# Modulation columns of the first layer in four quarters of two blocks, and the first four units computed two blocks at a time

## What is computed

```python
cond = jax.nn.silu(c.astype(jnp.float32))
mod = cond @ ada_w[i].astype(jnp.float32) + ada_b[i].astype(jnp.float32)
shift, scale, gate = jnp.split(mod[:, None, :], 3, axis=-1)
h = (rms_norm_f32(x, norm_g[i]) * (1.0 + scale) + shift).astype(x.dtype)
...
proj = h @ w_in
q, k, v, g = jnp.split(proj, [RET_QK_WIDTH, 2 * RET_QK_WIDTH, 2 * RET_QK_WIDTH + RET_WIDTH], axis=-1)
```

## Time and profile before

| | us |
|---|---|
| median of 3 runs | 1806.66 |
| lowest and highest | 1804.52, 1806.71 |
| profiled execution, its own time | 1805.74 |
| span of the profiled execution | 1803.9 |
| TensorE busy | 1763.1 (98% of the span) |
| VectorE, ScalarE, GpSimd busy | 931.5, 471.5, 1103.0 |

### The profile page before, as it was taken

How to read it: one execution, slowest core, us unless ns; L and a number is a source line. 1 busy time by engine, 2 the same in 40 slices (tenths; PEclk the granted TensorE clock), 3 DMA queues, 4 the chain that set the end, 5 groups by cost and what they waited for, 6 DMA issues and landing times.

```text
span 1803.9 us, 26195 instructions
## 1 busy us (share of the span) xinstructions
PE 1763.1 (98%) x9198; PEld 1477.0 (82%) x9198; DVE 931.5 (52%) x1534; ACT 471.5 (26%) x958; POOL 1103.0 (61%) x848
## 2 busy tenths in 40 slices
PE   6999999999999999999999999989989999999998
PEld 4888888888888888888888778877878878888887
DVE  4754736574455545555443888786373463213311
ACT  4121221200233222322221247555332422002200
POOL 3656555698455444645457659864066588667863
PEclk9999999999999999999999999999999999999999
DMA  9523222385232222332223322200022333333331
GB/s 359 171 77 94 84 73 76 93 302 166 62 105 81 77 76 77 92 91 76 75 77 104 96 73 59 59 24 25 24 82 76 88 95 103 101 98 88 99 99 54
DMA packets 281588, 172.87 MB, mean 96 GB/s; under 512 B 6000, under 2 KB 272560, under 8 KB 280496
## 3 DMA queue, kind: packets, MB, share of 16 engines
q1 hardware_dynamic: 275024, 151.01, 28.5%
q10 hardware_dynamic: 6496, 20.93, 3.4%
HBM read 169.69 MB, written 2.10 MB: 95 GB/s over the span
## 4 chain that ended last, share of the span: by engine, by line
PE 92%; DVE 6%; SPq 1%; ACT 1%; DMA 0%; issue 0%; DVEq 0%; ACTq 0%
PE acc L390 14%; PE acc L392 14%; PE acc L391 14%; PE ob L390 4%; PE ob L392 4%; PE ob L391 4%; PE acc L420 3%; PE acc L422 3%; PE acc L421 3%; PE sc L1622 2%; PE acc L438 2%; PE acc L439 2%; PE acc L440 2%; PE sc L1543 1%; PE ob L1634 1%; PE acc L2035 1%
## 5 line engine op out<-in xcount | busy, mean ns | idle before, releaser
L766 POOL TENSOR_TENSOR wl<-raw,wh 128x512 fp32r<-128x512 f32 x456 | 638.6, 1421 | 19.3
L763 POOL TENSOR_SCALAR wh<-raw 128x1024 fp32r<-128x1024 f32 (+1 forms) x232 | 268.4, 1157 | 571.2 <-PE acc L392 143.5
L390 PE MATMUL acc<-hh,wh 128*128 128x512 f32 x800 | 325.6, 407 | 1.2 <-ACT sq L1413 1.2
L392 PE MATMUL acc<-hh,wl 128*128 128x512 f32 x800 | 313.7, 392 | 0.0
L391 PE MATMUL acc<-hl,wh 128*128 128x512 f32 x800 | 312.8, 391 | 0.0
L390 PEld LDWEIGHTS acc<-hh,wh 128*128 128x128 f32 x800 | 151.3, 189 | 35.5 <-issue 2.6
L391 PEld LDWEIGHTS acc<-hl,wh 128*128 128x128 f32 x800 | 151.5, 189 | 32.3 <-issue 2.4
L392 PEld LDWEIGHTS acc<-hh,wl 128*128 128x128 f32 x800 | 150.9, 189 | 33.0
L390 PE MATMUL ob<-Yh,wh 128*128 128x512 f32 x256 | 100.5, 393 | 0.0
L392 PE MATMUL ob<-Yh,wl 128*128 128x512 f32 x256 | 99.7, 390 | 0.0
L391 PE MATMUL ob<-Yl,wh 128*128 128x512 f32 x256 | 99.7, 389 | 0.0
(11 more groups left out here) (545 smaller groups left out, 3725.7 us busy)
## 6 DMA issues: line engine op xcount, KB each, us to landing
raw<-in_att_w_in SPq DMA_DIRECT2D x64, 512.0 KB, 4.0
raw<-in_mlp_w SPq DMA_DIRECT2D x64, 512.0 KB, 3.9
raw<-in_ret_w_in SPq DMA_DIRECT2D x48, 512.0 KB, 3.7
ada_w<-in_ada_w ACTq DMA_DIRECT2D x8, 1536.0 KB, 7.0
raw<-in_w_in SPq DMA_DIRECT2D x23, 512.0 KB, 3.6
ada_w<-in_ada_w SPq DMA_DIRECT2D x16, 512.0 KB, 8.9
raw<-in_ret_w_out SPq DMA_DIRECT2D x16, 512.0 KB, 4.3
raw<-in_att_w_out SPq DMA_DIRECT2D x16, 512.0 KB, 4.0
```

The source lines that it names most:

```text
L390: e.matmul(bank[:, :], wh[:, s, k, :], rhs_high(k), start=(start and k == 0), stop=False)
L392: last = e.matmul(bank[:, :], wl[:, s, k, :], rhs_high(k), start=False, stop=(stop and k == k1 - 1))
L763: e.tensor_scalar(wh[:, s, 0:k1, :], raw[:, s, 0:k1, :], 1.0, 1.0, ALU.mult, ALU.mult).then_inc(high_done, 1)
L766: low = e.tensor_tensor(wl[:, s, k0:k0 + KT // 2, :], raw[:, s, k0:k0 + KT // 2, :], wh[:, s, k0:k0 + KT // 2, :].bitcast(F32), ALU.subtract)
```

## The change

The four parts are cut another way: part n now holds scale and shift of blocks 2n and 2n+1, 256 columns each. Each of the 16 transfers of 512 KB becomes two of 256 KB with rows of 1 KB. A part then gives both modulation vectors of two blocks (`ada_mod` with one addition over both and one gain). The loads of units 0 and 1 now both stand ahead of part 1, unit 2 ahead of part 2, and parts 2 and 3 follow one another. On TensorE the first four units are cut in pieces of two blocks. All columns go to the bank `st`, and `ada_turned(n)` waits for `mod0` of n-1.

```diff
             def load_ada0(n):
-                part, k0 = ADA_PART[n]
                 for j in range(KT // 2):
-                    e.dma_start(ada_w0[n][:, 2 * j:2 * j + 2, :],
-                                rows(ins["ada_w"][0], 2 * j, 2 * j + 2, part * D + k0 * P, S)).then_inc(ada_in[n][j], 16)
+                    for half in range(2):
+                        e.dma_start(ada_w0[n][:, 2 * j:2 * j + 2, half * 256:(half + 1) * 256],
+                                    rows(ins["ada_w"][0], 2 * j, 2 * j + 2, (1 - half) * D + 2 * n * P, 256))\
+                         .then_inc(ada_in[n][j], 16)
...
-            for n in range(1, 4):
-                load_ret(0, (n - 1,))
-                load_ada0(n)
+            load_ret(0, range(2))
+            load_ada0(1)
+            load_ret(0, (2,))
+            load_ada0(2)
+            load_ada0(3)
             load_ret(0, range(3, 6))
...
             ada_turned(0)
             norm_spread(e, "n0")
             ada_rows(1)
+            first_unit(0, 0, 2)
+            ada_turned(1)
+            first_unit(1, 0, 2)
+            ada_rows(2)
+            first_unit(0, 2, 4)
+            ada_turned(2)
+            first_unit(1, 2, 4)
+            ada_rows(3)
             e.wait_ge(*AC.at(f"x{2 * NT - 1}"))
-            ada_turned(1)
-            first_unit(0, 0, 4)
-            ada_rows(2)
-            ada_rows(3)
-            ada_turned(2)
-            first_unit(1, 0, 4)
+            first_unit(2, 0, 4)
             ada_turned(3)
-            first_unit(2, 0, 4)
             for j in range(3):
-                first_unit(j, 4, KT)
-            first_unit(3, 0, KT)
+                first_unit(j, 4, 6)
+            first_unit(3, 0, 6)
+            for j in range(4):
+                first_unit(j, 6, KT)
...
-            for k in range(4):
-                normed(k)
-            ada_mod(1)
-            for k in range(4):
-                low(k)
-            ada_mod(2)
-            for k in range(4, KT):
-                normed(k)
-            ada_mod(3)
-            for k in range(4, KT):
-                low(k)
+            for n in range(4):
+                if n:
+                    ada_mod(n)
+                for k in range(2 * n, 2 * n + 2):
+                    normed(k)
+                for k in range(2 * n, 2 * n + 2):
+                    low(k)
```

More of the change, by code:

```diff
@@ L223, in build @@
         ada_w0 = [at(f"ada_w0{n}", [P, KT, S], n * 16 * KB) for n in range(4)]
-        ADA_PART = [(1, 0), (0, 0), (1, 4), (0, 4)]
         ada_g0 = at("ada_g0", [P, KT, D], 0)
@@ L880, in _ @@
             e.activation(cos_[:, :], tmp[:, 1, :], ACT.Sin).then_inc(*AC.done("rope"))
-            ada_rows(1)
-            e.wait_ge(*V.at("mod01"))
             for k in range(KT):
-                if k == 4:
-                    ada_rows(2)
-                    ada_rows(3)
-                    e.wait_ge(*V.at("mod03"))
+                if k and k % 2 == 0:
+                    ada_rows(k // 2)
                 e.wait_ge(*V.at(f"n0t{k}"))
@@ L1437, in _ @@
                     last.then_inc(*PE.done(f"x{2 * t + half}"))
-            mod_bank = [st, ob[1], st, ob[1]]
             def ada_rows(n):
@@ L1446, in ada_rows @@
                     if k % 2 == 0:
-                        e.wait_ge(ada_in[n][k // 2], 16)
+                        e.wait_ge(ada_in[n][k // 2], 32)
                     g = k % 4
@@ L1453, in ada_turned @@
             def ada_turned(n):
-                part, k0 = ADA_PART[n]
-                c = part * KT + k0
                 e.wait_ge(*AC.at(f"rows{n}"))
-                if n >= 2:
-                    e.wait_ge(*V.at(f"mod0{n - 2}"))
+                if n:
+                    e.wait_ge(*V.at(f"mod0{n - 1}"))
                 for j in range(4):
-                    last = e.matmul(mod_bank[n][:, c + j:c + j + 1], sq[:, n % 2, j * P:(j + 1) * P], qk_gain[:, 2:3],
+                    c = (1 - j // 2) * KT + 2 * n + j % 2
+                    last = e.matmul(st[:, c:c + 1], sq[:, n % 2, j * P:(j + 1) * P], qk_gain[:, 2:3],
                                     start=True, stop=True)
@@ L1481, in _ @@
             ada_rows(1)
-            e.wait_ge(*AC.at(f"x{2 * NT - 1}"))
-            ada_turned(1)
-            first_unit(0, 0, 4)
-            ada_rows(2)
-            ada_rows(3)
-            ada_turned(2)
-            first_unit(1, 0, 4)
+            first_unit(0, 0, 2)
[6 more added lines that the diff above has]
+            ada_rows(3)
+            e.wait_ge(*AC.at(f"x{2 * NT - 1}"))
+            first_unit(2, 0, 4)
             ada_turned(3)
-            first_unit(2, 0, 4)
             for j in range(3):
-                first_unit(j, 4, KT)
-            first_unit(3, 0, KT)
+                first_unit(j, 4, 6)
+            first_unit(3, 0, 6)
+            for j in range(4):
+                first_unit(j, 6, KT)
             def ret_values(i, u, c):
@@ L2373, in _ @@
             roots(e, 0, NT, "n0root")
-            mod_bank = [st, ob[1], st, ob[1]]
             def ada_mod(n):
-                part, k0 = ADA_PART[n]
-                c = part * KT + k0
+                k0 = 2 * n
                 e.wait_ge(*PA.at(f"cols{n}"))
[L2381 to L2385, removed]
+                m = mod[:, 0, 0:2, k0:k0 + 2]
+                step(e, e.tensor_tensor(m, st[:, 0:2 * KT].rearrange("p (a k) -> p a k", a=2)[:, :, k0:k0 + 2],
+                                        sm("ada_b0", 0, 2 * KT).rearrange("p (a k) -> p a k", a=2)[:, :, k0:k0 + 2],
+                                        ALU.add), V, f"mod0{n}")
+                step(e, e.scalar_tensor_tensor(out=gain[:, 0, k0:k0 + 2], in0=mod[:, 0, 1, k0:k0 + 2], scalar=1.0,
+                                               in1=sm("norm_g0", k0, 2), op0=ALU.add, op1=ALU.mult), V)
             def normed(k):
```

## The result

| | us |
|---|---|
| median before, 20 runs | 1806.07 |
| median after, 20 runs | 1809.17 |
| after over before | 1.0017, 95% interval 1.0010 to 1.0024 |
| profiled execution after, its own time and its span | 1808.94, 1807.1 |

The change costs 3.1 us (1.8 to 4.3). That is a small loss, clear of the scatter, but under the bound of 0.2% (3.6 us) that the prediction set, so it counts as no change; the upper end of the interval lies beyond the bound. One of the 20 runs after took 7120.33 us; nothing here explains it, the ratio leaves it out, and the median of the other 19 is 1808.99 us. The mark set in the prediction, the first matmul of step three, moved from 64.84 us to 67.54 us, by 2.7 us. The spans differ by 3.2 us, so nearly all of the loss is in the first 68 us.

What follows compares the result with a forecast made beforehand. Start bound by TensorE's own work from 29 us; its 3.3 us gain is eaten by the slot hand-over (value product 0.3 us later), and interference makes step three 1.3 us later: 1805.9 becomes 1807.2 us, range 1804.1 to 1810.0.

Steps and rivals of the forecast that it cites:

- The verdict and the sign: Whole kernel: +1.3 us, slower but no change within 0.2% (3.6 us); chance of within 0.86.
- The likeliest case: Start up to step three: slot hand-over eats TensorE's gain, later arrival stays, full clock; +1.3 us, chance 0.45.
- rival 2: TensorE's idle stretch ahead of the value product: clock falls, its two tiles run slow; +1.3 to +3.3 us, chance 0.27.
- The arrival of the last part: Modulation weights' load: rows of 1 KB cost 16 x 0.083 = 1.3 us, last part at 38.2 us instead of 36.9.
- rival 1: Modulation weights' load: 1 KB rows cost nothing, part 3 at 36.9 us; 1804.9 to 1805.9 us, chance 0.15.
- 3 (40.9): Modulation weights' load: 1 KB rows as dear as 512 B or small transfers cost; +4.0 us, 1809.9, chance 0.10.
- The first slow stretch: TensorE near 26 us: the idle stretch goes and the slow clock with it, no idle stretch longer than 1.3 us.
- TensorE up to the first units' end: TensorE from part 3's arrival: 17.57 us of work, ending at 55.8 us against 59.09 before, a gain of 3.3 us.
- The hand-over of unit 0's slot: GpSimd starts unit 4 at 52.1 us, both units at 59.4; TensorE idles 3.6 us, value product 0.3 us later.
- The interference: GpSimd's units beside VectorE's rotation: unit 5 +0.3 us, unit 6 4.9 us; step three at 66.15 us, 1.3 us later.
- The clock: Value product's first two tiles behind TensorE's idle gap: priced at full clock, 5.75 us.
- Rival 4: Head of the value product: hand-over does not bind, full TensorE gain stands; -4.6 us, 1801.3, chance 0.03.

Runs made afterwards that it cites:

- e5: Kernel before, each 512 KB transfer of the modulation cut by columns into two with rows of 1 KB; one run, 1808.39 us.
- e6: Kernel before, each 512 KB transfer of the modulation cut into two of 256 KB that keep rows of 2 KB; one run, 1803.45 us.
- e1: Changed kernel, but units 0 to 2 run their last two blocks before all of unit 3, so unit 0 ends early; ratio 1.0003 to the kernel before.
- e7: Kernel of e3, with VectorE's rotation also waiting until units 4 to 7 are split; one run, no ratio, unit 6 took 3.64 us instead of 4.83.
- e2: Kernel before with only the changed kernel's order of the tail of the first units; ratio 1.0041 to the kernel before, +7.4 us.
- e3: Changed kernel with 14 unused matmuls ahead of the value product to keep TensorE busy; ratio 1.0011 to the kernel before, +2.0 us.
- e9: Kernel of e1 with unit 6 loaded ahead of the gate columns and unit 7 behind five of them; 1803.31 us, ratio 0.9986 to the kernel before.
- e4: Changed kernel with the unit loads where they stood before, one between parts; ratio 1.0017 to the kernel before, +3.1 us.

## Why the prediction was right, and where it was off

**The verdict and the sign held**, the size was short: +1.3 us forecast, +3.1 measured. 1809.17 us lies inside the range of 1804.1 to 1810.0 us, near its upper end. The likeliest case and rival 2 were one mechanism with and without the slow clock, and rival 2, which had 0.27, is what happened.

**The arrival of the last part: right in size, in part by luck.** 38.26 us, forecast 38.2. The term of 1.3 us, taken a third of the way between two rows, came out as 1.33 us with rows of 1 KB (e5), against rivals 1 (36.9) and 3 (40.9). But it was worked out as 0.083 us for each of 16 pieces. e5 has that price in parts 1 and 2 alone, none in part 0, and twice as much in part 3, of which 0.48 us came without the shorter rows too (e6). The two deviations cancel.

**The first slow stretch: right, and lucky.** It is gone, as said. The reason given was that no idle stretch there is longer than 1.3 us. In e1 and e7, whose start is that of after, the waits from 18 us on are no longer (1.04 us at most), and yet the clock was 0.50 for about 3 us. First e1, then after:

```profile
22.00:23.00 1.00, 1.00 (x6) 0.19 (x4) 0.87 (x2) 1.00 (x2) 1.00 (x2) 0.50 1.08 379
```

```profile
22.00:23.00 1.00, 0.71 (x6) 0.14 (x4) 0.87 (x2) 0.94 (x2) 0.98 (x1) 1.00 1.08 382
```

It cost e1 little: TensorE took the last piece of part 1 at 25.42 us, in after at 25.25 us.

**TensorE up to the first units' end: a term mis-sized.** I let the last four matmuls of the rows take 0.45 us, a share of a long run of them. The last piece arrives while TensorE waits for it, and from the arrival at 38.26 to the next work at 39.24 us it takes 0.98 us. The same was to be read in the kernel before, where four such matmuls behind a wait are busy for 1.05 us (at 21.93 and 23.28 us). That is 0.53 us; unit 2's 12 matmuls took 2.85 us instead of 2.72, and the rest is rounding. The columns ended at 42.91 us instead of 42.17, and unit 0's last matmul began at 52.33 us instead of 51.5. No matmul waited for a late block, as forecast.

**The hand-over of unit 0's slot: right in kind, late by that term.** GpSimd started unit 4 at 52.92 us, 0.59 us behind that matmul as in the earlier trace rows, where I had 52.1 us. TensorE idled 3.45 us (3.6 forecast), and the value product began at 60.25 us instead of 59.65. e1 and e2 show that the order of the tail moves unit 4 by 3.9 and 7.0 us with the transfers unchanged.

**The interference: right for units 6 and 7, not for unit 5.** The gate sums began at 46.42 us, not 45.5, mostly as the last modulation was 0.7 us later; so the rotation started at 59.35 us instead of 58.4. Its first instruction was slowed to 1.39 us, unit 5 was not (2.50 us for its low half). Unit 6 took 4.83 us, forecast 4.9. The high half of unit 7 was done at 66.55 us, forecast 66.15: 0.82 us for the later start of unit 4, less 0.32 for units 4 and 5 (7.23 us, forecast 7.55) and 0.10 for unit 6 and the high half of unit 7 (6.40 us, forecast 6.5).

**The clock: the step that failed.** The forecast priced the two tiles behind the gap at full clock, 5.75 us; the only row on its side was the 2.2 us of idle time at 1326 us. The clock fell to 0.50 at about 60.1 us, and the tiles took 7.29 us, 1.54 us longer, where rival 2 gave 2.7 us at most. Of this 1.0 us reached the end, 67.54 against 66.55 us, and e3 gives 0.93 us. The forecast wait of 0.75 us ahead of step three did not show, as the slow tiles ended behind the high half of unit 7. So the sum at step three is 1.3 + 0.4 + 1.0 = 2.7 us. The Trainium skill (TensorE: Matmul & The Clock Gate, HAM oscillation) describes this case, a burst that starts slow behind a wait for data, and here the trace agrees, with GpSimd in the place of the data: the rule deserved more than 0.27 for a gap longer than the 2.97 us that had brought the low clock at 28 us.

**Two slips in the working.** The stretch with only 8 one-column products ahead of the idle time at 26 us is 1.8 us long by the earlier trace rows (0.79 of waiting and 1.02), not 1.6. Rival 4's 54.5 us rests on an arrival at 36.9 us, which is rival 1's; with the forecast's own arrival it is 55.8 us, a gain of 3.3 us and not 4.6.

**What stays open.** The spans differ by 0.5 us more than step three does. Between 440 and 470 us both kernels have a slow stretch, of different length; windows of 10 us, before and then after:

```profile
440.00:450.00 10.00, 9.21 (x59) 8.62 (x60) 3.40 (x12) 0.63 (x1) 6.72 (x6) 0.88 0.38 111
450.00:460.00 10.00, 7.01 (x23) 5.23 (x22) 9.18 (x14) 5.41 (x8) 0.00 (x0) 0.61 0.16 47
460.00:470.00 10.00, 10.00 (x44) 8.01 (x44) 1.74 (x6) 2.60 (x5) 4.28 (x4) 1.00 0.16 51
```

```profile
440.00:450.00 10.00, 9.21 (x60) 8.36 (x61) 2.40 (x5) 0.63 (x1) 8.60 (x8) 0.96 0.54 153
450.00:460.00 10.00, 7.01 (x27) 5.92 (x27) 7.55 (x18) 3.48 (x5) 0.86 (x1) 0.50 0.18 52
460.00:470.00 10.00, 10.00 (x39) 8.12 (x38) 5.34 (x11) 2.41 (x4) 0.08 (x1) 0.85 0.17 49
```

The clock is lower in two of three windows after. Whether the shift of the start causes that or chance does wasn't tried. Runs of one kernel scatter by 3 to 5 us, and such stretches may be a part of that; it is argued, not shown.

## What to carry to other kernels

When pieces of work on the bound engine are put in another order, ask first which buffer each piece gives back and when: here the last use of unit 0's slot moved 30 matmuls nearer to the work that needs its successor, and that cost more than the idle time that the finer pieces saved. Finish one buffer's user after another at the end of such a block, not all of them together. Then follow the freed engine to its next input, since the gain stopped at a load queued behind 4 MB that nobody wanted yet (e1), and came only when that moved as well (e9).

## What the runs showed of the hardware that I had not expected

- An idle TensorE of 1.86 us was followed by a granted clock of 0.50 (e1), while 2.2 us at 1326 us had left it at 1.00, and at 21 us the same work with waits of 1.04 us at most had it at 0.50 in e1 and at 1.00 in after. The length of a gap alone does not tell whether the clock falls; in e1 it cost 1.7 us, about as much as the gap.
- After gaps of the same 3.45 us the clock was low up to 63.6 us in one kernel (after) and up to about 66 us in another (e4). The two tiles took 7.29 us in the one and 8.35 us in the other, so the price of such a gap differed by about a microsecond.
- The length of the rows had a price where the rule that I weighed gave none: 512 KB took 1.28 us in rows of 2 KB, by the prediction's working, and 0.083 us more in rows of 1 KB in two of the four parts (e5).
